# Retention: values and gate of a head by seven quarter products with the positions stationary, and a head's scores in the middle of the preceding head's output product

## The chip, the cores and the metric

The kernel runs on one core of a Trainium2 chip. The metric is the device time of one launch in microseconds, as the median of the runs shown. Engines are named as in the profile: PE (TensorE), DVE (VectorE), ACT (ScalarE), POOL (GpSimd), SP (SyncE, here only a queue of DMAs).

## What is computed

Two transformer blocks over 512 positions of width 1024, in 32-bit floats. The change lies in the first mixer of the second block, a retention with four heads:

```python
def _retention(h, w_in, gn_g, w_out):
    proj = h @ w_in                                  # 1024 x (1024 q, 1024 k, 2048 v, 2048 g)
    q, k, v, g = jnp.split(proj, [RET_QK, 2 * RET_QK, 2 * RET_QK + RET_VW], axis=-1)
    q = _rope(q, pos)
    k = _rope(k, pos) * (RET_DK ** -0.5)
    ...
    # per head: o = (q k^T * decay) v, over the chunk itself and all before it
    mu = jnp.mean(o, axis=-1, keepdims=True)
    var = jnp.mean(jnp.square(o - mu), axis=-1, keepdims=True)
    o = ((o - mu) * lax.rsqrt(var + EPS)).reshape(B, S, RET_VW) * gn_g
    y = jax.nn.silu(g) * o
    return y @ w_out
```

A head has 256 columns of q and of k, 512 of v and of g, and 512 rows of w_out.

## The kernel before

A 32-bit product is made from three: every operand is split into a high part in PE's reduced format and a low remainder, and a product is hi*hi + lo*hi + hi*lo (lines 688 to 690). Activations are split by ACT (high part) and DVE (remainder). Weights come by DMA in blocks of 1 MB (128 partitions x 2048 numbers); ACT makes the high half-blocks (`w_hi`, line 1198, 128x1024 each), POOL the remainders (`w_lo`, line 667). There are two such slots, so a block is converted while the block before it is multiplied: half a block for each unit of PE that ends (`after_unit`). A *unit* is 24 matmuls of 512 columns into one bank of PSUM (or two half units), `unit_done` counts finished units, and `unit_taken` those that DVE has read out; PE waits on it before it writes a bank again. All engines run their instructions in the order of the program text.

A head of the retention before is, on PE: 2 units of q, 2 of k; three units of values (`unit_value`, 1024 x 512 in two K halves); the scores (24 matmuls); the last unit of values; a unit of the gate; the mix (30 matmuls of scores with values); two units of the gate; 16 transposes of the normalised mix; the last unit of the gate; 4 units of the output product (`unit4`). DVE rotates q and k (`rope`), scales the scores, takes the statistics of the mix, normalises, gates and adds the output product into `x`. Heads 1 to 3 are a loop on PE and SP. Before head 0 the input is normed twice: `first_units` make q and k while the squares are summed, and `spread` puts a factor on all partitions by a product with diagonals (line 789); a second `spread`, whose diagonals DVE makes between the ropes of q and k, stands behind the first unit of values.

Elsewhere (`QUARTERS`, in the FFN and the MLPs) a 2x2 block product is already made by seven quarter products in place of eight. There the differences of weights that DVE makes lie in PSUM.

Of the kernel before, what the change touches and what calls it, by code (L numbers as in the profile page):

```python
# [24 lines left out]
P = 128  # L25
# [66 lines left out]
BLOCK_KINDS = {"mix": ["raw"] * 14, "ffn": (["raw"] * 8 + list(QUARTERS)) * 2 + ["raw"] * 10, "ret": ["raw"] * 32, "att": ["raw"] * 16,  # L92
# [3 lines left out]
LAST_TILES = [4, 6, 5, 7, 0, 2, 1, 3]  # L96

# [7 lines left out]
class Count:  # L105

    def __init__(self):
        self.n, self.turn, self.per = 0, None, 0  # L110

    def value(self, off=0):
        return self.n + off if self.turn is None else self.turn * self.per + (self.n + off)

    def beyond(self, k):

        return self.turn is not None or self.n > k


class Counts:  # L120
# [27 lines left out]
    def repeat(self, turns, body):  # L148

        every = [*self.of.values(), self.block, self.unit]  # L150
        before = [x.n for x in every]
        body(0)
        per = [x.n - b for x, b in zip(every, before)]
        if turns == 1:
            return
        with self.engine.Fori(1, turns) as i:
            for x, b, p in zip(every, before, per):
                x.n, x.per, x.turn = b, p, i
            body(i)
        for x, b, p in zip(every, before, per):  # L160
            assert x.n - b == p
            x.n, x.turn = b + turns * p, None


def build(nc, phases, x_in, w_in, w_out, w_gate, w_up, w_down, ret_w_in, ret_w_out, att_w_in,
# [4 lines left out]
    with ctx:  # L170
# [6 lines left out]
        hh = sb("hid_hi", [P, KT, SEQ], F32R)  # L177
        hl = sb("hid_lo", [P, KT, SEQ], F32R)
# [5 lines left out]
        with ExitStack() as early:  # L184
            combined = early.enter_context(nc.sbuf_tensor("combined", [P, 6144], F32R))
            down_0 = early.enter_context(nc.sbuf_tensor("down_0", [P, 2048], F32))
        qh = sb("q_hi", [P, 2, SEQ], F32R)
# [13 lines left out]
        with ExitStack() as early:  # L201
            work = early.enter_context(nc.sbuf_tensor("work", [P, 8448], F32))
            tap_w = early.enter_context(nc.sbuf_tensor("tap_w", [P, 4, 2, P], F32))
# [5 lines left out]
        bias_rows = nc.dram_tensor("bias_rows", (ATT_HEADS, EXT), F32).ap()  # L209

# [29 lines left out]
        cos, sin, decay = part(0, SEQ), part(512, SEQ), part(1024, RET_HEADS, SEQ)  # L240
        sg, o_sb, ptf = part(3072, 4, SEQ), part(5120, ST, SEQ), part(7168, PACKED)
# [128 lines left out]
        mix_ready = sem("mix_ready")  # L370

# [10 lines left out]
        for kind in plan:  # L382
            for _ in range(2):
                lows.append(lows[-1] + (kind not in ("t2", "t4")))
# [8 lines left out]
        def by_rows(b):  # L393

            return b >= rows_from and plan[b] in QUARTERS
# [8 lines left out]

        def first_turn(f):
            return plan[:begins(f)].count("b11")

        def begins(f):
            return sum(len(BLOCK_KINDS[g]) for g in phases[:phases.index(f)])
# [12 lines left out]
        def _(sp):  # L422
            c = Counts(sp, sems)

            def load(matrix, k0, nk, c0, width):
                slot = c.block.n % 2

                if c.block.turn is not None:
                    sp.wait_ge(w_lo, 2 * c.block.value(-1) + (lows[2 * raw_blocks[c.block.n - 2] + 2] - 2 * (c.block.n - 1)))
                elif c.block.n > 1:  # L430
# [22 lines left out]
            for f in phases:  # L453
# [55 lines left out]
                if f == "ret":  # L509
                    def head(h):  # L510
                        load(ret_w_in, 0, KT, h * 256, 256)
                        load(ret_w_in, 0, KT, h * 256 + 1024, 256)
                        for k0 in (0, 4):
                            load(ret_w_in, k0, 4, h * 512 + 2048, 512)
                        for c0 in (4096, 4352):
                            load(ret_w_in, 0, KT, h * 512 + c0, 256)
                        outs_k4(ret_w_out, h * 4)
                    c.repeat(RET_HEADS, head)
# [2047 lines left out]
```

## Time and profile before

| | us |
|---|---|
| median of 3 runs (1864.18 to 1864.57) | 1864.39 |
| profiled execution: span from first to last instruction | 1862.6 |
| runs' median less that span (start and end of a launch) | 1.8 |
| head 2 of the retention, from one load of its first block to the next head's | 99.4 |

The profiled execution's own launch time is not listed beside its span; the three runs lie within 0.4 us of each other, so their median less the span is taken for what lies around it. In the profile a busy PE is not PE at its peak, since matmuls overlap: what one costs on PE is read from the distance of the starts of two, not from its length. "Idle before" a row is the time in which its engine had nothing to run, with the instruction that ended it.

### The profile page before, as it was taken

The page shows a single profiled execution, that of the slowest core. Times are in us where ns is not written, and L with a number is a line of the kernel's source. Part 1 is how long each engine was busy: PE and PEld are TensorE (multiplying, and loading weights), DVE is VectorE, ACT ScalarE, POOL GpSimd, SP SyncE. Part 2 cuts the span into 40 slices and gives each one's busy share as a digit, 9 for nine tenths or more (in the row PEclk, how much of TensorE's full clock was granted, in tenths as well). Part 3 has the DMA queues.
Part 4 walks back from the last instruction along what each step waited for, and adds up shares of the span by engine and source line. Part 5 has one row for each costly group of instructions (what it writes and reads, how often), then busy time and mean ns, then how long its engine had stood idle before and what let it go on. Part 6 is the DMA issues. An engine that isn't in the chain of part 4 may idle for free.

```text
span 1862.6 us, 24027 instructions
## 1 busy us (share of the span) xinstructions
PE 1840.3 (99%) x9444; PEld 1569.4 (84%) x9444; DVE 1133.1 (61%) x1816; ACT 843.1 (45%) x1318; POOL 944.5 (51%) x407
## 2 busy tenths in 40 slices
PE   9999999999999999999999999999999999999998
PEld 7778889898888888888889898998888887888886
DVE  6987775775776333433565445457777766454546
ACT  5345343342354233332454545355666645443544
POOL 5673466475443434333448566574222327674755
PEclk9999999999999999999999999999999999999999
DMA  5222414424232222222243232403333332423221
GB/s 187 91 91 68 153 51 155 151 76 151 68 113 68 91 91 91 68 91 90 83 165 114 68 136 68 136 28 99 101 101 110 103 101 80 136 78 126 91 91 57
DMA packets 142764, 187.10 MB, mean 100 GB/s; under 512 B 4000, under 2 KB 102576, under 8 KB 142528
## 3 DMA queue, kind: packets, MB, share of 16 engines
q1 hardware_dynamic: 135392, 172.76, 28.1%
q10 hardware_dynamic: 7264, 12.86, 2.4%
q8 instruction: 72, 1.18, 0.3%
q14 instruction: 36, 0.29, 0.0%
HBM read 179.28 MB, written 6.33 MB: 100 GB/s over the span
## 4 chain that ended last, share of the span: by engine, by line
PE 80%; DVE 9%; ACT 3%; issue 1%; POOL 1%; DMA 0%; ACTq 0%; DVEq 0%
PE ps L688 26%; PE ps L690 26%; PE ps L689 26%; DVE ps L2066 1%; POOL w_lo L667 1%; ACT w_hi L1198 1%; DVE work L2408 1%; DVE diagonals L1734 1%; DVE xl L1760 0%; DVE probs_t_lo L2427 0%; PE ps L1077 0%; DVE work L2421 0%; PE ps L1011 0%; DVE work L2004 0%; DVE q_hi L2398 0%
## 5 line engine op out<-in xcount | busy, mean ns | idle before, releaser
L667 POOL TENSOR_TENSOR w_lo<-raw,w_hi 128x1024 fp32r<-128x1024 f32 x244 | 591.1, 2431 | 754.9 <-ACT w_hi L1198 754.9
L688 PE MATMUL ps<-xh,w_hi 128*128 128x512 f32 x1408 | 554.0, 393 | 4.9 <-DVE xl L1760 2.7
L690 PE MATMUL ps<-xh,w_lo 128*128 128x512 f32 x1408 | 548.2, 389 | 0.0
L689 PE MATMUL ps<-xl,w_hi 128*128 128x512 f32 x1408 | 548.2, 389 | 0.0
L1198 ACT ACTIVATE w_hi<-raw 128x1024 fp32r<-128x1024 f32 x262 | 273.2, 1057 | 427.9 <-PE ps L690 397.6
L688 PEld LDWEIGHTS ps<-xh,w_hi 128*128 128x128 f32 x1408 | 264.4, 188 | 64.4 <-issue 8.0
L689 PEld LDWEIGHTS ps<-xl,w_hi 128*128 128x128 f32 x1408 | 264.4, 188 | 55.3 <-issue 1.9
L690 PEld LDWEIGHTS ps<-xh,w_lo 128*128 128x128 f32 x1408 | 264.3, 188 | 55.3
L688 PE MATMUL ps<-hid_hi,w_hi 128*128 128x256 f32 (+1 forms) x688 | 228.3, 332 | 1.8 <-DVE hid_lo L2010 0.7
L690 PE MATMUL ps<-hid_hi,w_lo 128*128 128x256 f32 (+1 forms) x688 | 227.1, 330 | 0.0
L689 PE MATMUL ps<-hid_lo,w_hi 128*128 128x256 f32 (+1 forms) x688 | 227.0, 330 | 0.0
L688 PEld LDWEIGHTS ps<-hid_hi,w_hi 128*128 128x128 f32 x688 | 130.8, 190 | 14.9 <-DVE hid_lo L2010 1.9
L690 PEld LDWEIGHTS ps<-hid_hi,w_lo 128*128 128x128 f32 x688 | 130.8, 190 | 11.9
L689 PEld LDWEIGHTS ps<-hid_lo,w_hi 128*128 128x128 f32 x688 | 130.8, 190 | 11.8 <-issue 0.2
L667 POOL TENSOR_TENSOR w_lo<-down,w_hi 128x1024 fp32r<-128x1024 f32 x40 | 96.2, 2420 | 84.2 <-ACT w_hi L1198 84.2
L1975 DVE TENSOR_TENSOR x<-x,ps 128x512 f32<-128x512 f32 x84 | 56.9, 685 | 75.5 <-PE ps L690 75.4
L667 POOL TENSOR_TENSOR w_lo<-work,w_hi 128x1024 fp32r<-128x1024 f32 x36 | 86.3, 2411 | 13.0 <-ACT w_hi L1198 13.0
L2342 DVE SCALAR_TENSOR_TENSOR work<-ps,r_bc 128x512 f32<-128x512 f32 x64 | 43.6, 690 | 79.9 <-PE ps L690 79.9
L688 PE MATMUL ps<-w_hi,xh 128*128 128x512 f32 (+1 forms) x256 | 86.6, 338 | 0.7 <-DVE work L2227 0.7
L690 PE MATMUL ps<-w_hi,xl 128*128 128x512 f32 (+1 forms) x256 | 86.0, 336 | 0.0
L689 PE MATMUL ps<-w_lo,xh 128*128 128x512 f32 (+1 forms) x256 | 86.0, 336 | 0.0
L690 PE MATMUL ps<-combined,w_lo 128*128 128x256 f32 x288 | 81.5, 283 | 0.0
(272 smaller groups left out, 3095.8 us busy)
## 6 DMA issues: line engine op xcount, KB each, us to landing
raw<-in_mlp_w_dram SPq DMA_DIRECT2D x40, 1024.0 KB, 5.4
raw<-in_ret_w_in_dram SPq DMA_DIRECT2D x24, 1024.0 KB, 5.2
work<-in_mlp_w_dram SPq DMA_DIRECT2D x16, 1024.0 KB, 5.7
raw<-in_att_w_in_dram SPq DMA_DIRECT2D x12, 1024.0 KB, 5.5
raw<-in_w_gate_dram SPq DMA_DIRECT2D x11, 1024.0 KB, 5.3
raw<-in_w_up_dram SPq DMA_DIRECT2D x11, 1024.0 KB, 5.5
raw<-in_w_in_dram SPq DMA_DIRECT2D x9, 1024.0 KB, 5.1
raw<-in_ret_w_out_dram SPq DMA_DIRECT2D x8, 1024.0 KB, 5.1
```

The source lines that it names most:

```text
L667: nc.gpsimd.tensor_tensor(half_of(wl[:, b % 2, :], b, half), half_of(source, b, half), half_of(wh[:, b % 2, :], b, half).bitcast(F32), ALU ...
L688: nc.tensor.matmul(o, a[0], b[0], start=first, stop=False, skip_group_check=True)
L689: nc.tensor.matmul(o, a[0], b[1], start=False, stop=False, skip_group_check=True)
L690: return nc.tensor.matmul(o, a[1], b[0], start=False, stop=last, skip_group_check=True)
L1198: nc.scalar.activation(to, source, ACT.Copy).then_inc(w_hi, c.made(w_hi))
L1734: V.reciprocal(rough, root_rows).then_inc(dve_step, c.made(dve_step))
L1975: V.tensor_tensor(tiles, tiles, ps[:, where, :].rearrange("p (m c) -> p m c", m=2), ALU.add).then_inc(unit_taken, c.made(unit_taken))
L2066: V.scalar_tensor_tensor(total if last else acc, src, w, acc, ALU.mult, ALU.add).then_inc(signal, c.made(signal))
L2342: V.scalar_tensor_tensor(hval[:, u % 2, :], bank(), 0.0, r_bc[:, :], ALU.max, ALU.mult).then_inc(unit_taken, c.made(unit_taken))
L2408: V.tensor_tensor_reduce(probs[:, h % 2, BY_QUERY[i]:BY_QUERY[i] + n], ps[:, bk, at:at + n], bias[:, h % 4, SEQ - n:SEQ], 1.0, MASKED, ALU ...
```

## The change

The products of values and gate of a head are seen as one product of 512 positions x 1024 inputs with 1024 inputs x (512 gate, 512 values) columns, cut into 2x2 blocks each way: positions 0-255 and 256-511, inputs 0-511 and 512-1023, gate and value columns. Seven quarter products with sums of the operands replace the eight. Each quarter product (`head_quarter`) is two units of 12 matmuls, the positions stationary and 512 columns of weights moving.

- **Weights.** Four differences per head: `d1` and `d3` by POOL, `d2` and `d4` by DVE (`second_difference`, `fourth_difference`), in place in four 1 MB holders in SBUF; of `d2` and `d4` DVE makes the remainder too (`difference_lo`).
- **Positions.** Four sums of the input are made once before head 0 (`position_sum`, DVE), split (ACT, DVE), stored to DRAM and fetched again for every head, 1 MB each.
- **Results.** `keep_product`, `value_sum`, `gate_sum` and `gate_copy` (DVE) put the seven products together from four banks.
- **Order.** The rope of a head's q and k and its scores now lie inside the preceding head's output product. For head 0 they come first, between `h11` and `d1`. The second `spread` stands directly behind `first_units`. The loop over the heads is written out. The gate is applied before the transposes.

```diff
+HEAD_QUARTERS = ("h11", "d1", "h22", "d2", "d3", "h21", "d4")
+BY_VECTOR = ("t2", "t4", "d2", "d4")
...
+                if kind == "h11":
+                    for cut in (slice(0, 1024), slice(1024, 2048)):
+                        nc.gpsimd.tensor_tensor(first[:, cut], second[:, cut], first[:, cut], ALU.subtract).then_inc(d1_made, 1)
+                if kind == "h22":
+                    for cut in (slice(0, 1024), slice(1024, 2048)):
+                        nc.gpsimd.tensor_tensor(second[:, cut], fourth[:, cut], second[:, cut], ALU.subtract).then_inc(d3_made, 1)
...
+                    def head_quarter(kind, h):
+                        n0 = 2 * head_block("h11", h)
+                        for half in range(2):
+                            taken = {"h11": n0 - (1 if h else 2), "d1": n0, "h22": n0 + 3 + half, "d3": n0 + 7 + half, "d4": n0 + 9 + half}
+                            if kind in taken:
+                                pe.wait_ge(unit_taken, taken[kind])
...
+                    first_units(order, double=True)
+                    spread()
+                    for h in range(RET_HEADS):
+                        more = h < RET_HEADS - 1
+                        head_quarter("h11", h)
+                        if h == 0:
+                            head_scores()
+                        for kind in ("d1", "h22", "d2", "d3"):
+                            head_quarter(kind, h)
+                        pe.wait_ge(pt_ready, c.next(pt_ready, 4))
+                        head_mix(h, (0, 1))
+                        if not more:
+                            head_mix(h, (2, 3))
+                        head_quarter("h21", h)
+                        if more:
+                            head_mix(h, (2, 3))
+                        head_quarter("d4", h)
+                        if more:
+                            unit8(X, fresh=1, bank=0)
+                            unit8(X, fresh=1, bank=1)
+                        head_turn()
+                        if more:
+                            unit8(X, fresh=2, bank=2)
+                            unit8(X, fresh=3, bank=3)
+                        unit4(H, 4, ready=hid_ready, fresh=2 if more else 0)
+                        unit4(H, 4)
+                        if more:
+                            head_scores()
+                        unit4(H, 4)
+                        unit4(H, 4)
...
+                    def second_difference(h):
+                        for cut in (slice(0, 1024), slice(1024, 2048)):
+                            V.tensor_tensor(lent(h, 0)[:, cut], lent(h, 0)[:, cut], lent(h, 2)[:, cut], ALU.subtract).then_inc(d2_made, c.made(d2_made))
...
+                    def head(h, prepare=None):
+                        keep_product(0, sg[:, 0, :])
+                        keep_product(1, sg[:, 1, :])
+                        second_difference(h)
...
+                        keep_product(2, sg[:, 2, :])
+                        keep_product(3, sg[:, 3, :])
+                        difference_lo("d2", h)
...
+                        fourth_difference(h)
+                        if h == 0:
+                            scale_x(range(0, 4))
+                        dve.wait_ge(pt_ready, c.now(pt_ready))
+                        keep_product(2, third_added[0])
+                        keep_product(3, third_added[1])
+                        dve.wait_ge(*c.own())
+                        value_sum(0)
+                        value_sum(1)
...
+                        gated(0)
+                        gated(1)
+                        if not more:
+                            gate_copy(0)
+                            gate_copy(1)
+                        gated(2)
+                        gated(3)
...
+                    position_sum(0)
+                    position_sum(1)
+                    position_sum_lo(0)
+                    position_sum_lo(1)
+                    rope(qh, ql, 0)
+                    V.tensor_copy(ms, r1c).then_inc(to_curve, c.made(to_curve))
+                    refine_root()
+                    diagonals(rc2, spread=False)
+                    position_sum(2)
+                    position_sum(3)
+                    position_sum_lo(2)
+                    position_sum_lo(3)
+                    rope(kh, kl, 2, take_r1=True)
```

The pieces are, in this order: POOL's differences, the quarter product and the program of PE, the second difference and the program of a head on DVE, and DVE's start of the retention. The new kernel has other line numbers than the profile before.

PE at the start of the retention, from the last unit of `first_units` on; before, the second spread (L789) stands behind a unit of values:

```order
L688 MATMUL ps<-xh,w_hi 128x512 [waits unit_taken,w_lo]
...
L688 MATMUL ps<-w_hi,xh 128x512 [waits unit_taken,w_lo]
...
L789 MATMUL ps<-diagonals,ones 128x128 [waits stats_in]
L789 MATMUL ps<-diagonals,ones 128x128 x3
L688 MATMUL ps<-w_hi,xh 128x512 [waits unit_taken,w_lo]
```

The same place of the changed kernel (L858 is a matmul of a split product, L945 the spread):

```order
L858 MATMUL ps<-xh,w_hi 128x512 [waits unit_taken,w_lo]
...
L945 MATMUL ps<-diagonals,ones 128x128 [waits stats_in]
L945 MATMUL ps<-diagonals,ones 128x128 x3
L858 MATMUL ps<-w_hi,xh 128x512 [waits w_lo,unit_taken]
...
L858 MATMUL ps<-q_hi,k_parts 128x512 [waits qk_ready]
```

The spread has no unit of values ahead of it any more, and the scores of head 0 stand one quarter product (h11) behind it.

DVE at the same place, from the copy of the first factor to the diagonals of the second; before:

```order
L2213 COPY r_bc<-ps 128x512 [waits stats_done]
L2217 TENSOR_TENSOR work<-work,r_bc 128x512 [waits tab_landed,dve_step]
...
L2224 TENSOR_TENSOR work<-ps,work 128x512 [waits unit_done,dve_step]
...
L2229 TENSOR_TENSOR work<-work 128x512 [waits unit_taken]
L2230 TENSOR_TENSOR work<-work 128x512
L2237 TENSOR_TENSOR q_lo<-work,q_hi 128x1024 [waits to_hi,hi_made]
...
L1724 TENSOR_TENSOR diagonals<-ident,cols 128x512 [waits dve_step]
L2224 TENSOR_TENSOR work<-ps,work 128x512 [waits unit_done]
```

and of the changed kernel (L2530 and L2536 are the position sums and their remainders, L2485 to L2498 the rope):

```order
L2478 TENSOR_TENSOR work<-work,r_bc 128x512 [waits tab_landed,dve_step]
...
L2530 SCALAR_TENSOR_TENSOR work<-x,prm,work 128x256 [waits scaled_x,dve_step]
...
L2530 SCALAR_TENSOR_TENSOR work<-x,prm,work 128x256 [waits sum_made]
...
L2536 TENSOR_TENSOR hid<-work,hid 128x1024 [waits sum_made,sum_hi] x2
L2485 TENSOR_TENSOR work<-ps,work 128x512 [waits unit_done]
...
L2490 TENSOR_TENSOR work<-work 128x512 [waits unit_taken]
L2491 TENSOR_TENSOR work<-work 128x512
L2498 TENSOR_TENSOR q_lo<-work,q_hi 128x1024 [waits to_hi,hi_made]
...
L1985 TENSOR_TENSOR diagonals<-ident,cols 128x512 [waits dve_step]
```

Eight sums and two remainders stand ahead of the rope of q, and so ahead of the diagonals; the other half of them follows the diagonals, ahead of the rope of k.

DVE in head 1, between the additions of head 0's last output unit and the first sum for the values; of before there stand only the ropes, the remainders of the values and the scores:

```order
L2229 TENSOR_TENSOR work<-work 128x512 [waits unit_taken]
L2230 TENSOR_TENSOR work<-work 128x512
L2237 TENSOR_TENSOR k_parts<-work,k_parts 128x1024 [waits to_hi,hi_made]
L2326 SCALAR_TENSOR_TENSOR hid_lo<-ps,cols,hid_hi 128x512 [waits hi_made,unit_done,qk_ready]
L2326 SCALAR_TENSOR_TENSOR hid_lo<-ps,cols,hid_hi 128x512
```

and of the changed kernel (in this order: two kept products of h11, the second difference, two of d1, the remainder of d2, the fourth difference, two of h22, the first sum):

```order
L2586 COPY work<-ps 128x512 [waits unit_done] x2
L2561 TENSOR_TENSOR raw<-raw,holder_0 128x1024 [waits holder_landed2,w_lo]
L2561 TENSOR_TENSOR raw<-raw,holder_0 128x1024
L2586 COPY work<-ps 128x512 [waits unit_done] x2
L2575 TENSOR_TENSOR w_lo<-raw,w_hi 128x1024 [waits w_hi] x2
L2568 TENSOR_TENSOR raw<-raw 128x1024 [waits d_lo,holder_landed0]
L2568 TENSOR_TENSOR raw<-raw 128x1024
L2586 COPY work<-ps 128x512 [waits unit_done,pt_ready]
L2586 COPY work<-ps 128x512 [waits unit_done]
L2593 TENSOR_TENSOR ps<-ps,work 128x512 [waits unit_done,unit_taken]
```

Six operations on 128x1024 with both inputs in SBUF now stand between the readings of PSUM that PE waits for.

## Rows read from the trace of the kernel before

**Rows 1.** The page, busy time of the engines.

```profile
PE 1840.3 (99%) x9444; PEld 1569.4 (84%) x9444; DVE 1133.1 (61%) x1816; ACT 843.1 (45%) x1318; POOL 944.5 (51%) x407
```

**Rows 2.** Stretch, head 2: us, busy of PE, PEld, DVE, ACT, POOL, clock, DMA.

```profile
706.85:806.28 99.43, 99.43 (x456) 83.00 (x455) 37.45 (x64) 32.22 (x41) 38.33 (x16) 1.00 0.26 85
```

**Rows 3.** Whom PE waited for, retention: us in total, times, longest.

```profile
PE ps L688 <- DVE work L2227: 0.7, 1, 0.7
```

**Rows 4.** Timeline of PE in head 1: start us, us, operation, [idle before].

```profile
707.07 1.91 PE L1011 MATMUL ps<-ident,work 128*128 128x128 f32 x16
...
708.73 0.48 PE L688 MATMUL ps<-xh,w_hi 128*128 128x512 f32 x1
...
714.28 0.39 PE L688 MATMUL ps<-hid_hi,w_hi 128*128 128x512 f32 x1
...
719.72 0.39 PE L688 MATMUL ps<-hid_hi,w_hi 128*128 128x512 f32 x1
```

**Rows 5.** Timeline of PE at the start of the retention.

```profile
557.06 0.39 PE L688 MATMUL ps<-w_hi,xh 128*128 128x512 f32 x1
...
562.50 1.05 PE L789 MATMUL ps<-diagonals,ones 128*128 128x128 f32 x8
...
564.27 0.47 PE L688 MATMUL ps<-w_hi,xh 128*128 128x512 f32 x1 [0.71 <-DVE work L2227]
```

**Rows 6.** Timeline of DVE at the start of the retention.

```profile
551.14 0.69 DVE L2224 TENSOR_TENSOR work<-ps,work 128x512 f32<-128x512 f32 x1
...
556.08 1.23 DVE L2237 TENSOR_TENSOR q_lo<-work,q_hi 128x1024 fp32r<-128x1024 f32 x1 [1.13 <-ACT q_hi L1216]
...
557.35 0.17 DVE L2249 COPY cols<-cols 128x4 f32<-128x4 f32 x1
...
558.80 2.93 DVE L1724 TENSOR_TENSOR diagonals<-ident,cols 128x512 f32<-128x512 f32 x1
```

**Rows 7.** Two stretches where DVE and POOL both read two tensors in SBUF.

```profile
514.54 2.71 DVE L1760 SCALAR_TENSOR_TENSOR xl<-x,prm,xh 128x512 fp32r<-128x512 f32 x1
...
567.84 9.32 DVE L2255 TENSOR_TENSOR x<-x,sum_of_squares 128x512 f32<-128x512 f32 x8
...
514.31 2.40 POOL L667 TENSOR_TENSOR w_lo<-raw,w_hi 128x1024 fp32r<-128x1024 f32 x1 [0.82 <-ACT w_hi L1198]
...
571.22 5.39 POOL L667 TENSOR_TENSOR w_lo<-raw,w_hi 128x1024 fp32r<-128x1024 f32 x2 [7.26 <-ACT w_hi L1198]
```

**Rows 8.** Groups of DVE: busy us, mean ns, idle before.

```profile
L1827 DVE TENSOR_TENSOR combined<-ps,combined 128x256 fp32r<-128x256 f32 x16 | 6.8, 425 | 22.1 <-ACT combined L1525 22.1
...
L2283 DVE TENSOR_SCALAR work<-work,cols 128x512 f32<-128x512 f32 x4 | 1.9, 544 | 0.0
```

**Rows 9.** Groups of ACT in head 2.

```profile
L1198 ACT ACTIVATE w_hi<-raw 128x1024 fp32r<-128x1024 f32 x16 | 16.7, 1056 | 36.0 <-PE ps L690 36.0
...
L1476 ACT ACTIVATE hid_hi<-ps,cols 128x512 fp32r<-128x512 f32 x4 | 2.5, 686 | 6.5 <-PE ps L690 6.5
...
L1492 ACT ACTIVATE work<-work 128x512 f32<-128x512 f32 x3 | 1.9, 633 | 9.2 <-DVE work L2002 9.2
...
L1492 ACT ACT_TABLE_LOAD x1 | 1.3, 1283 | 0.0
```

**Rows 10.** Group of POOL in head 2.

```profile
L667 POOL TENSOR_TENSOR w_lo<-raw,w_hi 128x1024 fp32r<-128x1024 f32 x16 | 38.3, 2404 | 61.1 <-ACT w_hi L1198 61.1
```

**Rows 11.** DVE's first reading of a unit after its last matmul.

```profile
719.92 1.29 DVE L1816 TENSOR_TENSOR x<-x,ps 128x512 f32<-128x512 f32 x2 [1.86 <-PE ps L690]
```

**Rows 12.** PE's last matmul, the clock after it, the launch's first matmuls.

```profile
1854.60 0.39 PE L690 MATMUL ps<-w_hi,hid_lo 128*128 128x512 f32 x1
...
1860.00:1861.00 1.00, 0.00 (x0) 0.00 (x0) 0.15 (x1) 0.00 (x0) 0.00 (x0) 0.67 0.63 248
...
L796 PE MATMUL ps<-ones x28: 274/421/580, 1.0 to 6.9; 128*128 128x128 f32 x28
```

More of the change, by code:

```diff
@@ L96, with begins_of @@
 LAST_TILES = [4, 6, 5, 7, 0, 2, 1, 3]
+def begins_of(phases, f):
+    return sum(len(BLOCK_KINDS[g]) for g in phases[:phases.index(f)])
 def taps_after(u):
@@ L408, in begins @@
         def begins(f):
-            return sum(len(BLOCK_KINDS[g]) for g in phases[:phases.index(f)])
+            return begins_of(phases, f)
         def next_prep(f):
@@ L710, in unit8 @@
                 w = weights(slot, 256)
+                bank = c.unit.n % banks[0] if bank is None else bank
                 for k in range(nk):
@@ L972, in _, with head_operand @@
                 if f == "ret":
-                    def head(h, first=False):
-                        if first:
-                            first_units(order, double=True)
-                        else:
-                            for n in range(4):
-                                unit8(X, fresh=(1, 2, 2, 3)[n])
-                        for n in range(3):
-                            unit_value(n)
-                            if first and n == 0:
-                                spread()
+                    def head_operand(kind, k, cut):
+                        if kind in SUM_SLOT:
+                            return sum_operand(kind, k, cut)
+                        k0, at = {"h11": (0, 0), "h21": (4, 0), "d4": (4, 256)}[kind]
+                        return [t[:, k0 + k, at + cut.start:at + cut.stop] for t in X]
@@ new lines, in value_tile_hi, with copy_mixed @@
+                    def value_tile_hi(h, s):
+                        act.wait_ge(unit_taken, 2 * head_block("h11", h) + 7 + s)
+                        if h == 0:
+                            act.wait_ge(sums_stored, 64)
+                        bank = (2, 3, 4, 5)[s]
+                        nc.scalar.activation(hh[:, 4 + s, :], ps[:, bank, :], ACT.Copy, scale=rc[:, s:s + 1]).then_inc(v_hi, c.made(v_hi))
+                    def copy_mixed(tiles):
+                        for i in tiles:
+                            act.wait_ge(mixed_done, c.next(mixed_done))
+                            nc.scalar.activation(o_sb[:, i, :], ps[:, 6 + i % 2, :], ACT.Copy).then_inc(o_copied, c.made(o_copied))
@@ L1494, in head @@
-                        after_unit()
-                        for i in range(ST):
-                            act.wait_ge(mixed_done, c.next(mixed_done))
-                            nc.scalar.activation(o_sb[:, i, :], ps[:, 6 + i % 2, :], ACT.Copy).then_inc(o_copied, c.made(o_copied))
-                        act.wait_ge(unit_taken, c.unit.value(0))
-                        nc.scalar.activation(sg[:, 0, :], sg[:, 0, :], ACT.Silu).then_inc(curve_made, c.made(curve_made))
-                        make_root()
@@ L1513, in _ @@
+                    qk_hi_of(kh)
+                    for h in range(RET_HEADS):
+                        head(h, None if h < RET_HEADS - 1 else nxt)
                 if f in ("mlp0", "mlp1"):
```

639 lines of the change are left out of this document (446 added, 193 removed).

## The prediction, made before the changed kernel had run

> **What bounds the kernel now.** First the page: PE is busy 99% of the span [rows 1]. Then one stretch of the loop: PE is busy in all of its 99.43 us at the full clock, DVE in 37, POOL in 38 [rows 2]. Then the waits of PE: in the whole retention it waited once, 0.7 us [rows 3]. So PE bounds this stage, and the other engines are hidden with room to spare. The step between matmuls comes from PE's timeline: 24 of them start at 714.28 and the next 24 at 719.72, so one costs 5.44/24 = 0.227 us and a quarter product or unit 5.44 us [rows 4]. Sixteen transposes take 1.66 us (707.07 to 708.73). The scores have 24 narrower matmuls: 99.43 less 414 x 0.227 (93.9) less 1.66 leaves 3.9 us.
>
> **What goes away.** Values and gate cost 192 matmuls per head, the seven quarter products 7 x 24 = 168. Four heads save 96 x 0.227 = 21.8 us of PE. The old 0.7 us wait behind the spread goes too [rows 5]. Together 22.5 us, if PE never waits. The rest asks where it must.
>
> **The port.** DVE gets about ten operations per head that read two tensors from SBUF. Rows show what these cost beside POOL [rows 7]. POOL starts at 514.31 and ends at 516.71; a DVE operation issued at 514.54 ends at 517.25, 0.54 later, instead of after 0.74. In the second stretch eight such operations take 9.3 us, where 0.6 each would be 4.8; POOL's two take 5.39, where 2.40 each is usual [rows 10]. So the two engines take turns, one instruction each. Operations that read one side from PSUM do not show this: the additions to x keep 0.69 [rows 11]. Beside a POOL that has work without a gap, a 128x1024 operation of DVE (1.23 alone, [rows 6]) costs 2.4 of waiting plus 1.1, and POOL loses 1.1.
>
> **A head from 1 on, from its h11 = 0.** h11 ends at 5.44, d1 at 10.88. ACT converts d1 once the last output unit ended (0.2 to 2.2, 1.0 per half, [rows 9]), POOL makes its remainder from 1.3 to 6.1, then goes on with h22 at once. DVE has kept the two products of h11 at 6.25 (a unit can be read 0.2 after its end, [rows 11]), and finds the port taken. From 6.05 on the two alternate: six POOL halves (h22, the difference d3, the remainder of d3) and six DVE halves (second difference, remainder of d2, fourth difference), 6 x 2.4 + 6 x 1.1 = 21.0, so until 27.05. The second difference ends after two of each, at 13.05; only then does DVE read bank 2 (0.69), and h22, which adds onto that bank, starts at 13.85 instead of 10.88: a wait of 3.0. h22 and d2 end at 24.73. d3 adds onto banks that `value_sum(0)` must have read: 27.05, two copies and the sum, 29.2, so a wait of 4.5. Later parts fit: the fetches of sums and blocks, the remainder of h21 (to 31.9), the ropes. The transposes have no room left (about 63.3 for both sides). A head costs 7.5 more, 2.1 net.
>
> **Head 0.** PE ends `first_units` at 557.06 [rows 5]. DVE starts the rope at 551.14 in the old kernel [rows 6]; now eight sums come first (128x256: 0.425 each, [rows 8], 0.38 from start to start, 3.1) and two remainders (2.5): rope at 556.7, its four PSUM products to 559.3. By then POOL works on h11 and d1: the subtraction ends at 562.0, the addition at 564.9, the remainder of q behind one more POOL half at 568.4. Root and refinement (557.35 to 558.80) give 569.9, the diagonals 0.7 more. The spread, before hidden behind a unit of values, starts at 570.75: a wait of 13.7. Spread and h11 take 6.2, to 576.95. DVE makes the other sums and remainders (to 576.1), rotates k beside the remainder of d1 (581.75), and ends k's remainder at 584.2: the scores wait 7.3. They end at 588.2, d1 at 593.65. By the same turns the second difference ends at 591.2; two scores and one remainder more, and bank 2 is read at 595.0: 1.4. d2 then ends at 605.9. DVE has the rest of the scores (to 601.2), the fourth difference, four scalings of x by turns with POOL's d3 and h21 (to 615.4), and only then `value_sum(0)`, at 617.4: 11.5. Sum 33.9.
>
> **Head 3.** The 7.5 as in the others. Its whole mix stands ahead of h21, so the third row waits for the last value: ACT converts half of d4 after d3 (1.25), then two value tiles (0.69 [rows 9], 2.55), DVE the remainder (3.4), against 2.0 of mix: 1.4. At the end no units of q and k cover the gating. From the end of d4: DVE's first gating ends at 1.2 behind POOL, the second at 1.8, the two copies at 3.05, ACT's two silu at 3.15 and 3.75 (0.63 each; the table, 1.28, is in), then two gatings by turns with POOL's last block, 7.7. Transposes at 7.8, then 0.6 until the first tile is split. 8.4. Sum 17.3.
>
> **The clock.** PE's last matmul ends at 1855.0; the granted clock is a mean 0.67 between 1860 and 1861, so it fell from 1.0 to 0.5 (2.4 to 1.2 GHz) at 1860.3, after 5.3 us of rest [rows 12]. Four of the new waits are longer. What the return costs, no wait in this trace shows. Nearest row: the first 28 matmuls of the launch take 6.2 us, where transposes of that shape need 2.9, so 3.3 lost. Bounds 0 and 4 x 3.3 = 13; two of the four fall ahead of another wait that hides them, so I take 2 x 2 = 4.0.
>
> **Sum.** -22.5 + 33.9 + 2 x 7.5 + 17.3 + 4.0 = +47.7. Against the profiled execution's span, 1862.6, that is 1910.3; the runs' median lies 1.8 over that span, so 1912. A difference under 3.7 us (0.2%) is no change here.
>
> **A rule against it.** The trace shows DVE's four normalisations at 0.544 us each, one tensor from SBUF, never beside POOL [rows 8]. The Trainium skill, VectorE: DVE Perf Modes, section The perf-mode tier table, has such 32-bit scalar operations use both read ports, and GPSIMD Engine Reference, section Key points, counts that as contention with POOL too; no row here shows it. As a mechanism of this kernel: if the normalisations take turns as well, the transposes of heads 0 to 2 come about 1.5 late each, +4.6, so 1917.
>
> **Rivals.**
> - *The port does not bind here* (not slower). If POOL and DVE ran side by side, the turns above vanish: heads 1 and 2 wait for nothing, the spread waits 8.0, the scores 5.2, d3 of head 0 1.4, head 3 1.4 + 4.9. That is 20.9, less 22.5, and about 1 for the clock: 1864. For it: DVE and POOL are each busy under 40% of a head [rows 2], so most of the time one of them is free. Against it: both stretches of [rows 7], where each slowed the other as soon as both had work. It decides if second differences end within 2.5 us of their start.
> - *DVE keeps the port for both halves.* Then the second difference ends at 10.65 and the first wait is 0.6; head by head 2.4 less, in head 0 about 5 less: 1900. Against it: the eight scalings lost the port to both POOL halves.
> - *The clock stays down longer.* With 3.3 lost at each long wait and some at the waits of 3.0 and 4.5 too: 4 x 3.3 + 6 x 1.5 = 22 instead of 4, so 1930. Against it: those short waits end below the 5.3 us of [rows 12].
> - *The change does less than it says*: the sums arrive late from DRAM and hold d2 or d3. For it: 18 MB more to move (four sums stored once, fetched in every head but for what is still at hand: 4 + 14). Against it: DMA is busy 0.26 of a head [rows 2], and d3's sum has 10 us. Each late fetch costs a few us: 1920.
>
> **How the numbers follow.** Forecast 1912 (1902 to 1922 by itself) 0.48; the normalisations take turns, 1917, 0.10; DVE keeps the port, 1900, 0.12; clock, 1930, 0.08; late sums, 1920, 0.05; the port does not bind, 1864, 0.10; between that and the forecast, with turns at only some places, 0.07. The port rival lies on the old time and is split between faster and no change (0.05 each); of the cases between, 0.02 may come within 0.2%: 0.05 faster, 0.07 the same, 0.88 slower. The range leaves out the port rival and what lies above the clock rival: 1877 to 1931.
>
> **What would show it.** Right: on PE, four long waits, for the diagonals (some 14 us), for k's remainder (7), for `value_sum(0)` of head 0 (11) and for the gating of head 3 (8); in heads 1 and 2 two waits of 3 and 4.5 released by a copy and by the first sum; DVE's SBUF operations of 128x1024 at a mean near 3 us; a clock under 1.0 behind the long waits. Wrong: those operations at 1.23 while POOL is busy, or a period of the loop near 94 us, which is 99.43 less 5.44.

## The result: 55 us slower, and the profile after

The changed kernel takes 1919.74 us (median of 4 runs, 1913.91 to 1921.6) against 1864.36: 1.0291 times as long, 95% interval 1.0277 to 1.0306. The forecast was 1912, 7.7 us less, with a range that holds the time. The profiled execution took 1919.85, with a span of 1918.0, 55.4 over the span before.

The page's line of busy time, the answer to [rows 1]: PE is no longer busy 99% of the span, though its busy time fell by only 3 us; DVE and POOL gained 144 and 79.

```profile
PE 1837.6 (96%) x9348; PEld 1561.8 (81%) x9348; DVE 1276.7 (67%) x1908; ACT 876.2 (46%) x1350; POOL 1023.9 (53%) x431
```

Whom PE waited for in the retention of the new kernel (us in total, times, longest). [rows 3] had one wait, of 0.7:

```profile
PE ps L858 <- DVE ps L2593: 19.3, 4, 9.2
PE ps L1198 <- DVE work L2629: 13.1, 4, 7.3
PE ps L945 <- DVE diagonals L1985: 13.0, 1, 13.0
PE ps L858 <- DVE work L2586: 7.6, 3, 2.5
PE ps L858 <- DVE k_parts L2498: 4.4, 1, 4.4
PE ps L858 <- DVE hid L2601: 1.1, 1, 1.1
```

All 58.5 us are waits for DVE. From the top: d3 for the first value sum (9.2 in head 0, 3.36 in each other head); the transposes for the gating (1.92 in heads 0 to 2, 7.35 in head 3); the spread for the diagonals; h22 of heads 1 to 3 for the copies of d1's products; head 0's scores for the remainder of k; head 3's mix for the values.

The stretch from the transposes of head 0 to those of head 1, as in [rows 2]:

```profile
654.17:756.92 102.75, 94.94 (x430) 78.25 (x431) 71.48 (x83) 38.94 (x47) 58.65 (x23) 1.00 0.37 126
```

Before, a head took 99.43 us, with DVE busy in 37 and POOL in 38. Now PE's work is 5 us shorter, but DVE is busy in 71 and POOL in 59, and the head is 3.3 longer. How much of DVE's 34 us more is work and how much is time in which POOL holds it, the first experiments tell.

That is seen in the timeline of head 1 (start, us, engine, line, operation). DVE's rows first, then POOL's of the same stretch:

```profile
698.69 6.67 DVE L2561 TENSOR_TENSOR raw<-raw 128x1024 f32<-128x1024 f32 x2
705.28 1.27 DVE L2586 COPY work<-ps 128x512 f32<-128x512 f32 x2
706.48 5.55 DVE L2575 TENSOR_TENSOR w_lo<-raw,w_hi 128x1024 fp32r<-128x1024 f32 x2
712.14 6.58 DVE L2568 TENSOR_TENSOR raw<-raw,holder 128x1024 f32<-128x1024 f32 x2
...
719.95 1.30 DVE L2593 TENSOR_TENSOR ps<-ps,work 128x512 f32<-128x512 f32 x2
...
704.23 6.72 POOL L844 TENSOR_TENSOR work<-raw,work 128x1024 f32<-128x1024 f32 x2
711.61 6.02 POOL L824 TENSOR_TENSOR w_lo<-work,w_hi 128x1024 fp32r<-128x1024 f32 x2 [0.66 <-ACT w_hi L1415]
```

The second difference (L2561), the remainder of d2 (L2575) and the fourth difference (L2568) take 6.67, 5.55 and 6.58 for two halves of 1.23 alone [rows 6]; POOL's difference takes 6.72 for two of 2.40 [rows 10]. The copies out of PSUM (L2586) keep 0.6 each, but stand behind them. On PE, h22 starts when they are done:

```profile
703.10 0.39 PE L860 MATMUL ps<-w_hi,hid 128*128 128x512 f32 x1
706.01 0.50 PE L858 MATMUL ps<-w_hi,hid 128*128 128x512 f32 x1 [2.53 <-DVE work L2586]
706.35 0.40 PE L859 MATMUL ps<-w_lo,hid 128*128 128x512 f32 x1
...
720.70 0.50 PE L858 MATMUL ps<-w_hi,hid 128*128 128x512 f32 x1 [3.36 <-DVE ps L2593]
```

The starts lie 2.91 apart for a wait of 2.53 and a step of 0.227, and the next step is 0.34: a restart of PE costs 0.27 besides the wait.

One place was only a rival in the prediction, and came. DVE's root and normalisation in the same head, with one operation of the statistics ahead of them, and POOL's remainders of that stretch:

```profile
735.50 0.69 DVE L2615 BATCH_NORM_STATS2 cols<-work 128x6 f32<-128x512 f32 x1
...
745.16 0.16 DVE L2510 TENSOR_TENSOR cols<-cols 128x4 f32<-128x4 f32 x1
745.36 2.42 DVE L2512 TENSOR_SCALAR cols<-cols 128x4 f32<-128x4 f32 x1
747.81 2.33 DVE L2514 TENSOR_TENSOR cols<-cols 128x4 f32<-128x4 f32 x1
750.18 3.99 DVE L2623 TENSOR_SCALAR work<-work,cols 128x512 f32<-128x512 f32 x4
...
735.42 4.78 POOL L824 TENSOR_TENSOR w_lo<-raw,w_hi 128x1024 fp32r<-128x1024 f32 x2 [12.15 <-ACT w_hi L1415]
745.34 4.78 POOL L824 TENSOR_TENSOR w_lo<-work,w_hi 128x1024 fp32r<-128x1024 f32 x2 [5.14 <-ACT w_hi L1415]
```

An operation on four numbers a partition that takes 0.17 elsewhere took 2.42: it waited for POOL's first half, the next one for the second. The four normalisations take 3.99 instead of 1.92. The statistics beside POOL keep their 0.69. The rule of the Trainium skill that the prediction weighed (VectorE: DVE Perf Modes, The perf-mode tier table; GPSIMD Engine Reference, Key points) agrees with these rows. The Trainium skill, SBUF — State Buffer, section Who interferes with whom, says that whoever issues first has the shared pair of ports for its whole instruction; the 2.42 us agree, for POOL had started at 745.34 and DVE at 745.36.

The clock, in windows of this kernel with the columns of [rows 2]:

```profile
584.00:589.00 5.00, 5.00 (x15) 4.42 (x16) 5.00 (x4) 0.36 (x1) 5.00 (x2) 0.50 0.30 125
616.00:620.00 4.00, 3.87 (x9) 3.10 (x10) 3.84 (x8) 1.28 (x2) 0.00 (x0) 0.50 0.54 209
...
825.00:828.00 3.00, 3.00 (x9) 2.33 (x8) 0.76 (x2) 0.00 (x0) 1.00 (x1) 0.50 0.21 36
...
963.30:968.00 4.70, 4.69 (x19) 4.45 (x20) 2.54 (x4) 2.76 (x4) 0.00 (x0) 0.50 0.00 0
```

PE works at 1.2 GHz in each of them, and in the same way from 570.15 and from 930.6: behind the four long waits, but also soon after the waits of 3.36 in heads 2 and 3 had ended, at 823.43 and 929.45 (a third such stretch, near 863, follows the wait of 1.92 of the transposes in head 2). Only three of these waits are longer than 5.3 us. With the matmuls' steps of 0.43 in place of 0.227 these stretches cost half their length: 2.75 behind the spread's wait, 2.8 behind the scores', 1.95 behind d3's, 2.45 behind that of the last transposes, and 3 x 1.7.

### The profile page after: what moved, and what is told of

Its sections match the earlier page's. It is cut to its first block, busy times and chain, and to the rows that moved or that the text cites. A ratio compares the mean times of both kernels' runs of the same rounds, so it can differ in the third digit from the quotient of the medians.

```text
span 1918.0 us, 23957 instructions
## 1 busy us (share of the span) xinstructions
PE 1837.6 (96%) x9348; PEld 1561.8 (81%) x9348; DVE 1276.7 (67%) x1908; ACT 876.2 (46%) x1350; POOL 1023.9 (53%) x431
## 4 chain that ended last, share of the span: by engine, by line
PE 73%; DVE 15%; ACT 4%; issue 2%; POOL 1%; ACTq 0%; DVEq 0%
PE ps L858 24%; PE ps L860 23%; PE ps L859 23%; DVE ps L2327 1%; POOL w_lo L824 1%; ACT w_hi L1415 1%; DVE raw L2561 1%; DVE work L2623 1%; DVE probs_t_lo L2824 1%; PE ps L1198 1%; DVE diagonals L1995 1%; DVE work L2818 1%; DVE x L2639 0%; DVE xl L2021 0%; ACT work L1875 0%
## 5 line engine op out<-in xcount | busy, mean ns | idle before, releaser
L824 POOL TENSOR_TENSOR w_lo<-raw,w_hi 128x1024 fp32r<-128x1024 f32 x216 | 530.2, 2464 | 621.3 <-ACT w_hi L1415 621.3
L858 PE MATMUL ps<-xh,w_hi 128*128 128x512 f32 x1280 | 505.3, 395 | 4.1 <-DVE xl L2021 1.9
L860 PE MATMUL ps<-xh,w_lo 128*128 128x512 f32 x1280 | 499.4, 390 | 0.0
L859 PE MATMUL ps<-xl,w_hi 128*128 128x512 f32 x1280 | 499.2, 390 | 0.0
L858 PEld LDWEIGHTS ps<-xh,w_hi 128*128 128x128 f32 x1280 | 240.8, 188 | 59.4 <-issue 8.5
L858 PE MATMUL ps<-hid,w_hi 128*128 128x256 f32 (+1 forms) x688 | 229.0, 333 | 2.2 <-DVE att_v L2778 1.1
L860 PE MATMUL ps<-hid,w_lo 128*128 128x256 f32 (+1 forms) x688 | 227.3, 330 | 0.0
L859 PE MATMUL ps<-hid,w_hi 128*128 128x256 f32 (+1 forms) x688 | 227.2, 330 | 0.0
L858 PEld LDWEIGHTS ps<-hid,w_hi 128*128 128x128 f32 x688 | 131.1, 191 | 15.2 <-DVE hid L2271 1.9
L860 PEld LDWEIGHTS ps<-hid,w_lo 128*128 128x128 f32 x688 | 130.9, 190 | 12.1
L859 PEld LDWEIGHTS ps<-hid,w_hi 128*128 128x128 f32 x688 | 131.1, 191 | 11.7 <-issue 0.2
L858 PE MATMUL ps<-w_hi,hid 128*128 128x512 f32 x224 | 90.9, 406 | 29.3 <-DVE ps L2593 19.3
L860 PE MATMUL ps<-w_hi,hid 128*128 128x512 f32 x224 | 89.3, 398 | 0.0
L859 PE MATMUL ps<-w_lo,hid 128*128 128x512 f32 x224 | 89.2, 398 | 0.0
L824 POOL TENSOR_TENSOR w_lo<-holder,w_hi 128x1024 fp32r<-128x1024 f32 x20 | 51.4, 2586 | 66.0 <-ACT w_hi L1415 66.0
```

What stands on the lines that cost most here:

```text
L824: nc.gpsimd.tensor_tensor(half_of(wl[:, b % 2, :], b, half), half_of(source, b, half), half_of(wh[:, b % 2, :], b, half).bitcast(F32), ALU ...
L858: nc.tensor.matmul(o, a[0], b[0], start=first, stop=False, skip_group_check=True)
L859: nc.tensor.matmul(o, a[0], b[1], start=False, stop=False, skip_group_check=True)
L860: return nc.tensor.matmul(o, a[1], b[0], start=False, stop=last, skip_group_check=True)
```

## The experiments

All ran in three rounds beside the kernel before (1864.4 to 1865.0). The first four tell apart why DVE is late.

**POOL's part of the port, in the quarter products.**

```diff
-nc.gpsimd.tensor_tensor(half_of(wl[:, b % 2, :], b, half), ...
+nc.gpsimd.tensor_tensor(few(half_of(wl[:, b % 2, :], b, half)), ...   # few: 64 columns where kind in HEAD_QUARTERS
...
-for cut in (slice(0, 1024), slice(1024, 2048)):      # d1 and d3
+for cut in (slice(0, 64), slice(1024, 1088)):
```

> POOL's remainders of h11, h22, d3, h21 and d1 and its two differences per head are made on 64 of 1024 columns (the rest is left out); DVE does all it did. Theory (DVE and POOL take turns at SBUF): the waits of h22 and d3 in heads 1 to 3 go (3 x (2.8 + 3.6) = 19 us), the spread waits some 5 less, the scores and head 0's d3 are late by 8 to 12 less, part of the clock comes back: about 1880 (1872 to 1890), DVE's second difference at 1.23 a half instead of 3.3. Rival (DVE has simply too much to do between the readings of PSUM, POOL does not matter): within 5 us of 1920, second difference as before.

Measured: 1879.6 (1878.1 to 1882.1), 1.0085 of the old kernel (1.0068 to 1.0102). Its waits of PE, and DVE's second difference by shape (busy, mean ns of a half):

```profile
PE ps L1199 <- DVE work L2630: 13.1, 4, 7.3
PE ps L946 <- DVE diagonals L1986: 8.0, 1, 8.0
```

```profile
L2562 DVE TENSOR_TENSOR raw<-raw,holder 128x1024 f32<-128x1024 f32 x2 | 2.5, 1284 | 0.0
```

DVE does the same work in the same order, and the waits of h22 and of d3 in heads 1 to 3 are gone, 17.7 us; a half of the difference takes 1.28 in place of 3.3. In head 0 the waits are 14.4 us shorter (the spread 5.0, the scores 1.0, d3 8.4), and 7 us of lower clock, behind d3 of head 0 and behind the short waits, are gone as well. Over the stretch from transposes to transposes:

```profile
636.84:733.11 96.27, 94.35 (x430) 78.43 (x431) 58.85 (x83) 38.80 (x47) 25.80 (x23) 1.00 0.39 134
```

DVE is busy in 58.9 us of 96.3 with all its work, against 71.5 of 102.8: 12.6 us of its busy time were POOL's turns. So DVE was not short of time, it was kept from SBUF. The 13.1 for the gating stay, as they must: they lie beside POOL's other blocks.

**POOL's part, in the blocks of q, k and the output.**

```diff
+few = (lambda v: v[:, 0:64] if kind in HEAD_QUARTERS else v[:, 0, 0:64]) if kind == "own" else (lambda v: v)
...   # few() as in the run before
```

> POOL's remainders of the q, k and output blocks of the heads are made on 64 columns (the rest is left out); all else as changed. Theory with the wider form of the port (scalar operations and the 128x4 ones of the root take turns as well): the three waits of the transposes, 1.9 us each, go, and the last head's wait before its transposes falls from 7.3 to about 4: 10 us less, 1910 (1906 to 1913). Rival (only operations with two tensors from SBUF take turns): the transposes keep their waits, only the last head gains, 1916.

Measured: 1905.3 (1901.0 to 1909.5), ratio 1.0226 (1.0209 to 1.0243). Its waits:

```profile
PE ps L859 <- DVE ps L2594: 12.6, 2, 9.2
...
PE ps L1199 <- DVE work L2630: 4.2, 1, 4.2
```

and the 128x4 operations and the normalisation:

```profile
L2513 DVE TENSOR_SCALAR cols<-cols 128x4 f32<-128x4 f32 x5 | 1.3, 268 | 0.2
L2515 DVE TENSOR_TENSOR cols<-cols 128x4 f32<-128x4 f32 x5 | 0.8, 163 | 0.2
L2624 DVE TENSOR_SCALAR work<-work,cols 128x512 f32<-128x512 f32 x16 | 7.7, 542 | 0.1
```

The wider form of the port holds: with POOL's instructions short, the 128x4 operations take 0.16 and 0.27, the normalisation 0.54, the transposes of heads 0 to 2 don't wait and those of head 3 wait 4.2. It gained 14, not 10: in the profiled execution, the fastest of the four, the waits of d3 in heads 1 and 2 went too, which the theory had not said. A later run, pool_behind_gate, shows the same, and its trace shows why.

**PE's order at the start.**

```diff
-spread()
 for h in range(RET_HEADS):
     head_quarter("h11", h)
     if h == 0:
+        spread()
         head_scores()
```

> PE's second spread stands behind h11 of head 0 instead of ahead of it. Theory (head 0's start is set by DVE's chain to the remainder of k, at 583.7 us of the span, and PE's 13.0 us wait for the diagonals only lies over it): the wait moves to the scores, the scores start within 1 us of 583.8, the time stays within 4 us of 1920. Rival (the spread's wait is itself the loss, since h11 could have run in it): 5 to 9 us faster, 1911 to 1915.

Measured: 1923.3 (1919.1 to 1925.4), ratio 1.0312 (1.0295 to 1.0330). The waits of the start:

```profile
PE ps L858 <- DVE k_parts L2498: 11.4, 1, 11.4
...
PE ps L945 <- DVE diagonals L1985: 4.5, 1, 4.5
PE ps L858 <- DVE work L2488: 2.1, 1, 2.1
```

The 13.0 and 4.4 became 2.1, 4.5 and 11.4; the scores start at 584.23 instead of 583.77. The 13 us in front of the spread are not a loss of their own: DVE's chain to the remainder of k is what PE waits for, in either order. The clock fell twice in head 1 here, near 722 and 760, where it did not in the change's profiled execution; at 1.7 us each these falls cover the 2.8 us by which this execution's span is longer.

**DVE's order.** In heads 1 to 3 the third kept product stands between the halves of the second difference, and a half of the fourth difference behind each of the first two value sums; in head 0 all scalings of x come later:

```diff
-second_difference(h)
 if h == 0:
+    second_difference(h)
     ...
-keep_product(2, sg[:, 2, :])
+    keep_product(2, sg[:, 2, :])
+else:
+    second_difference(h, (0,))
+    keep_product(2, sg[:, 2, :])
+    second_difference(h, (1,))
 keep_product(3, sg[:, 3, :])
 ...
-fourth_difference(h)
 if h == 0:
-    scale_x(range(0, 4))
+    fourth_difference(h)
 ...
 value_sum(0)
+if h:
+    fourth_difference(h, (0,))
 value_sum(1)
+if h:
+    fourth_difference(h, (1,))
 ...
-    scale_x(range(4, KT))
+    scale_x(range(KT))
```

> On DVE in heads 1 to 3 the third kept product stands between the halves of the second difference, the fourth difference behind the first value sums (half behind each); in head 0 all scalings of x stand behind the second remainder of the values. Nothing is left out. Theory (turns at SBUF delay the readings of PSUM that stand behind the differences): h22 waits under 0.7, the first value sums come at once, but the remainder of d2 is late now and d2 waits some 2; head 0's d3 waits under 1.5 instead of 9.2. 3 x 4 + 8 + 3 of clock = 23 less: 1897 (1890 to 1904). Rival (DVE is short of time as a whole in these stretches): the waits move on to d2, d3 and d4, under 10 us less.

Measured: 1891.1 (1890.8 to 1892.7), ratio 1.0144 (1.0128 to 1.0161): 29 us gained by order alone. The waits that changed:

```profile
PE ps L858 <- DVE w_lo L2575: 4.9, 3, 1.6
...
PE ps L858 <- DVE ps L2593: 0.3, 1, 0.3
```

27 us of waits for L2593 and L2586 became 0.3, and the remainder of d2 is late instead, 1.64 a head. The lower clock behind short waits is gone with them.

**The position sums.**

```diff
-V.scalar_tensor_tensor(out_[:, k, :], in_, scale, other[:, k, :], ALU.mult, op)
+V.scalar_tensor_tensor(out_[:, k, 0:16], in_[:, 0:16], scale, other[:, k, 0:16], ALU.mult, op)
...   # and the remainders in the same way
```

> DVE's sixteen position sums and their four remainders before head 0 are made on 16 columns of a tile (the rest is left out). Theory (the start of head 0 is one chain on DVE, 551 to 584 us of the span): 5 us less ahead of the rope of q, which then runs before POOL has work, and 5 less ahead of the rope of k: the spread waits under 6 instead of 13.0, the scores start 10 to 14 us earlier, and the time falls by 12 to 16: 1906 (1902 to 1910). Rival (the sums lie beside POOL's or ACT's work that sets the end anyway): under 4 us.

Measured: 1912.5 (1909.6 to 1918.0), ratio 1.0262 (1.0242 to 1.0282): 7 us, half of what the theory said, and not all of it is the chain's. Head 0's scores start at 579.82 instead of 583.77, 4 us earlier; the rest of what the profiled execution gained (it is the fastest of the four) lies in heads 1 to 3, where d3 does not wait any more, for a reason that pool_behind_gate shows. PE's first matmul of the scores, then DVE and POOL ahead of it:

```profile
579.82 0.80 PE L858 MATMUL ps<-q_hi,k_parts 128*128 128x512 f32 x1 [3.19 <-DVE k_parts L2498]
...
563.90 2.19 DVE L2725 COPY cols<-cols 128x4 f32<-128x4 f32 x1
...
560.11 5.95 POOL L838 TENSOR_TENSOR holder<-work,holder 128x1024 f32<-128x1024 f32 x2
```

The rope of q came 2.7 us earlier, not 5 (DVE now waits for ACT's high parts of the sums), and POOL came 1.7 earlier as well, since ACT converts its block behind those sums: the rope takes its turns still (1.33 and 2.82 for two additions of 0.6), and even the copy of four numbers takes 2.19, until POOL's second half of d1 is done at 566.06. The chain on DVE is what sets the start, but of the 10 us of work that the theory took from it, 4 came back at the scores.

**The clock.** Dummy products in the four long waits:

```diff
+pe.wait_ge(sum_made, 4)
+keep_warm(105, 5)
 spread()
```

(and 55, 75 and 58 in the other three)

> Dummy products of 128 columns fill most of PE's four long waits (105 ahead of the spread, 55 ahead of head 0's scores, 75 ahead of its d3, 58 ahead of head 3's transposes); nothing else is changed. Theory (the lower clock behind these waits costs, but in head 0 DVE's chain hides what it costs ahead of the next wait): the clock stays at its upper level behind them, and 1.9 at d3 and 2.4 at the transposes come back, 4 to 5 us: 1915 (1913 to 1917). Rival (all of the lower clock's loss behind the four is on the path, 2.7 + 2.8 + 1.9 + 2.4): 1910. If the clock doesn't depend on PE's rest: 1920.

Measured: 1938.1 (1933.4 to 1945.8). A mistake of mine, and so no verdict: a product of 128x128 in this type shows as two matmuls (x210 for 105), and they ran past the waits.

```profile
557.16 23.61 PE L952 MATMUL ps<-ones 128*128 128x128 f32 x210
```

105 products took 23.6 us, 0.224 each. Again with numbers by that row, 52, 27, 45 and 29 in the same places:

> As kept_warm, with dummies sized by its rows (0.224 us each: a product of this type is two passes): 52, 27, 45 and 29, so that each ends before what PE waits for. Theory (behind the two long waits whose cost nothing hides, the clock costs 1.9 and 2.4; the rest lies ahead of waits on DVE): 4.5 to 6.5 less than 1920, 1914 (1912 to 1916). Rival (all 9.8 us of the loss behind the four is on the path): 1910 or less. Without dependence of the clock on PE's rest: 1920.

Measured: 1914.6 (1910.1 to 1919.2), ratio 1.0269 (1.0246 to 1.0291): by the medians 5.1 us less than the change, as the theory has it, but the runs of the two overlap (the change took 1913.9 to 1921.6), so the times alone do not decide between 5 and 10. Its clock behind the scores' wait (behind the other three it reads 1.00 as well):

```profile
584.00:589.00 5.00, 5.00 (x30) 4.53 (x31) 5.00 (x4) 0.41 (x1) 5.00 (x2) 1.00 0.32 133
```

The two traces decide it, for both have the same three falls behind short waits. Scores and spread start where they did (583.83, 570.24): there the lower clock cost nothing. The first addition of x behind the last head starts at 968.48 for 973.12, 4.6 earlier.

**POOL later, nothing left out.**

```diff
+if kind == "own" and half == 0:
+    name, h = own_at[b]
+    if name == "k" and h or (name, h) == ("o1", RET_HEADS - 1):
+        pool.wait_ge(p_ready, 4 * (h if name == "k" else h + 1))
```

> POOL makes the remainder of the next head's k block only when the four gatings are done (in the last head that of the second output block); nothing is left out. Theory (DVE's root and normalisation take turns with just these remainders): the root's 128x4 operations take 0.17, the waits of the transposes in heads 0 to 2 go (3 x 2.1), the last head's wait falls by 2 to 3, and a little clock: 9 us less, 1911 (1907 to 1914). Rival (the k block comes too late for its own unit): the units of k wait up to 3 us a head and the gain is gone.

Measured: 1902.0 (1901.4 to 1902.5), ratio 1.0196 (1.0179 to 1.0213). Root and normalisation of head 1 there:

```profile
740.33 0.17 DVE L2516 TENSOR_SCALAR cols<-cols 128x4 f32<-128x4 f32 x1
...
740.74 1.92 DVE L2627 TENSOR_SCALAR work<-work,cols 128x512 f32<-128x512 f32 x4
```

Only POOL's time was moved, and the waits of the transposes in heads 0 to 2 are gone; that of head 3 is 4.5. It gained 17.7 where 9 were said; 6.7 of the rest are the waits of d3 in heads 1 and 2 again. Their trace in head 1 (start of h22 on PE, the stretch behind it with its clock of 0.51, ACT's high part of d3, the fourth difference on DVE, POOL's remainder of d3):

```profile
702.95 0.50 PE L862 MATMUL ps<-w_hi,hid 128*128 128x512 f32 x1 [2.53 <-DVE work L2590]
...
704.00:707.00 3.00, 3.00 (x9) 2.32 (x8) 3.00 (x2) 0.00 (x0) 3.00 (x2) 0.51 0.36 147
...
709.03 1.06 ACT L1419 ACTIVATE w_hi<-work 128x1024 fp32r<-128x1024 f32 x1 [5.58 <-PE ps L864]
...
709.05 4.60 DVE L2572 TENSOR_TENSOR raw<-raw,holder 128x1024 f32<-128x1024 f32 x2
...
710.17 5.75 POOL L828 TENSOR_TENSOR w_lo<-work,w_hi 128x1024 fp32r<-128x1024 f32 x2 [2.31 <-ACT w_hi L1419]
```

and ACT's high part of d3 in the change, where h22 starts at 706.01:

```profile
710.47 1.06 ACT L1415 ACTIVATE w_hi<-work 128x1024 fp32r<-128x1024 f32 x1 [3.96 <-PE ps L860]
```

Here the clock fell over h22; in the change it fell behind the wait of d3 (heads 2 and 3) or in neither place (head 1). ACT waits for PE within h22, so its high part of d3 came 6.08 us behind the start of h22 instead of 4.46. POOL stood idle for 2.31 in place of 0.66, DVE had a free turn, the fourth difference took 4.60 for 6.58, and the first value sum was done before PE came to d3. Such a fall costs PE some 1.7 us; over h22 it saves a wait of 3.36. This is not POOL's new timing: in sums_narrow, with POOL's work as in the change, the clock fell over h22 in heads 1 to 3, and d3 waits in none of them. So some 7 of the 17.7 us came from the place where the clock fell, which no edit chose, and some 11 from POOL's later work. Why it fell there is open.

**All together.** The edits of vector_order (with the fourth difference of head 0 late as well), pool_behind_gate and kept_warm; the lines show what is new against these:

```diff
-if h == 0:
-    fourth_difference(h)
+keep_warm(105, 5)      # as in kept_warm, ahead of the spread; 70 ahead of the scores, 40 ahead of the last transposes
```

> The order on DVE of the run vector_order (in head 0 the fourth difference late as well), POOL behind the gate, and dummy products in the waits ahead of the spread, of head 0's scores and of the last transposes; nothing is left out. Theory, adding the parts: 1891 less 6.5 for the transposes, 4.5 for the last head with its clock, 2.5 in head 0: 1877 (1871 to 1883), still above the old kernel, since the start of head 0 on DVE stays. Rival (the parts feed one another's waits): 1885 or more.

Measured: 1901.8 (1901.1 to 1902.2); the dummies of this one were sized like those of the first kept_warm and overran. With 52, 27 and 13:

> As combined, with 52, 27 and 13 dummies. In combined the dummies ran over: head 0's scores began 19 us after k's remainder was there, the last transposes 3.7 after the gating. Theory: 1902 - 19 - 3.7 = 1879 (1875 to 1883), still slower than the old kernel: what remains is the start of head 0 (13 and 7 us of waits) against the 21.8 us saved. Rival (the overrun hid waits of d3 and h22 in head 0 that come back): 1885 or more.

Measured: 1880.0 (1879.7 to 1881.6), ratio 1.0085 (1.0068 to 1.0102), the clock at 1.0 in the whole retention. Its waits besides the dummies (11.8, 6.2 and 3.1 us of them):

```profile
PE ps L862 <- DVE w_lo L2586: 5.0, 3, 1.7
...
PE ps L1203 <- DVE work L2640: 1.5, 1, 1.5
```

40 of the 55 us are back, and it is still 15.6 slower than the old kernel: 34 us of waits and dummies, 21 of them in head 0 up to h22, against the 21.8 saved. No version faster than the old kernel was found. One with head 0 in the old order would save 16.3 and keep the other 13 of waits and 2 to 3 of restarts: an estimate from these rows, about level, and not tried.

## Why the prediction was right, step by step

| step | forecast | measured |
|---|---|---|
| PE's work, and the old 0.7 | -22.5 | -21.5 (head 1: 102.75 less 7.8 of waits and 0.7 of restarts is 94.2, 5.2 under 99.4; four times that, and the 0.7) |
| head 0: spread, scores, h22, d3 | 13.7 + 7.3 + 1.4 + 11.5 = 33.9 | 13.0 + 4.4 + 0 + 9.2, and 2.75 + 2.8 of lower clock between them: 32.2 |
| heads 1 to 3: h22 and d3 | 3.0 + 4.5 each, 22.5 | 2.53 + 3.36 each, 17.7 |
| transposes, heads 0 to 2 | 0 (rival: 4.6) | 5.8 |
| head 3: values, gating | 1.4 + 8.4 | 1.1 + 7.35 |
| clock, besides head 0's row | 4.0 | behind d3 of head 0 and the last transposes 1.95 + 2.45, behind short waits 3 x 1.7: 9.5 |
| restarts | 0 | 14, 0.27 each, 0.16 at transposes: 3.3 |

The measured column adds up to 55.4. The first addition of x behind the last head lies at 973.12 for 918.77, 54.35 later, so the terms are good to some 1 us; 1.0 more comes in the attention behind it, where PE's waits for k_odd (1.0 for 0.3) and att_v (1.1 for 0.7) are longer. Why they are is open. The 7.7 that the forecast missed by is what remains of 15.6 too little (transposes, clock, restarts, PE's work) and 7.9 too much (head 0, h22 and d3, head 3), so that the sum came so near is in part luck.

- **The port** was the right mechanism, and the two POOL runs show it against the rival that had the old time (1864) as its end: same work on DVE, short instructions on POOL, and 40 us are gone. That DVE keeps the port for both halves is refuted by 6.67 for two. One row was read for more than it shows: POOL was idle from 719.27 to 721.06 in the old kernel, so the additions to x of [rows 11], from 719.92 on, do not stand beside it. The new kernel shows what was meant: its two value sums at 719.95 keep 1.30 beside a POOL that is busy from 717.59 to 723.27.
- **Head 0** came out as the sum (1.7 under it) and not term by term. The lower clock behind the spread stretched h11 and the scores and so took from the waits for DVE behind them; the instants set by DVE were forecast well (k's remainder ready at 584.2, measured 583.7; the first value sum done at 617.4, measured 616.0).
- **The step that failed is the normalisation.** I put "the transposes have no room left" and charged nothing, holding the port of one-input operations for a rival at 0.10. It is shown by pool_own_narrow and pool_behind_gate: 1.92 a head, and most of it in two operations on four numbers that I had not counted at all.
- **The clock** was sized about right where it was expected, and left out elsewhere. 4.0 was said for the long waits that nothing hides; the stretches behind them give 4.4, and kept_warm_short 4.6. What I left out are the falls behind short waits, 5.1 more: I had read the 5.3 us of [rows 12] as a rest that must be passed, but the clock fell behind waits of 4.4, 3.4 and 1.9 too, and within the four long waits it fell 4.9, 3.1, 2.9 and 2.0 us after PE's last matmul.
- **Too much for h22 and d3**, by 4.8, or 1.6 a head: the stretch of turns, from 698.69 to 718.72, took 20.0 where 21.0 were said, and two restarts, which the table counts by themselves, are 0.54 of the starts. POOL has a gap of 0.66 ahead of d3's remainder, and a turn is nearer 3.3 than 3.5.

## What to carry to other kernels

Before work is given to an engine that looks half idle, ask what it reads beside whom: DVE operations with two inputs in SBUF, and scalar ones however small, each waited for one whole POOL instruction here (2.4 us), and what counts is what stands behind them in order. Where they can't be avoided, put the reading that PE waits for between the halves, and let POOL start later: those two moves gave back 29 and some 11 us (18 measured, 7 of them by the place where the clock fell), with nothing left out. And reckon a saving of PE's work against the first head of a loop by itself, where the preparation has no PE work to hide it.

## What the runs showed of the hardware that was not expected

- DVE operations on 128x4 took 2.2 to 2.4 us beside POOL (TENSOR_SCALAR, TENSOR_TENSOR and COPY, 0.16 to 0.17 alone), while BATCH_NORM_STATS2 kept 0.69.
- PE's clock fell to 1.2 GHz in the middle of work, 1.2 and 1.4 us behind a wait of 3.36 and 1.1 behind one of 1.92, and in only some of the heads that had the same waits.
- Where it falls can matter more than that it falls: over h22 it cost PE some 1.7 us and saved a wait of 3.36. The change's four runs spread over 7.7 us; what spreads them is not shown, for pool_behind_gate, with three such falls, spread over 1.1, as little as vector_order and combined_short (1.9 each), which had none in the heads of the loop.
- A 128x128 product of float32 is two rows of PE, 0.112 us each.
